# The first adaLN columns of a decoder trunk: summed on VectorE, or multiplied on TensorE as they land

## The reference, cut to what matters

```python
c_act = jax.nn.silu(c)
for l in range(DEPTH):
    cond = c_act @ w_ada[l] + b_ada[l]
    sh_a, sc_a, ga_a, sh_m, sc_m, ga_m = [v[:, None, :] for v in jnp.split(cond, 6, axis=-1)]
    h = rmsnorm(x, g_mix[l]) * (1.0 + sc_a) + sh_a
    z = h @ w_in[l] + b_in[l]
    ...
```

## Time and profile before

| what | value |
|---|---|
| median of 3 runs | 3387.36 us (3386.69 to 3388.49) |
| the profiled execution's own time | 3386.8 us |
| its span | 3385.0 us |
| mean granted TensorE clock | 0.984 |
| TensorE busy | 3240.5 us, 96% |
| VectorE busy | 1612.0 us, 48% |
| GpSimd busy | 1338.4 us, 40% |
| ScalarE busy | 787.6 us, 23% |

### The profile page before, as it was taken

How to read it: one execution, slowest core, us unless ns; L and a number is a source line. 1 busy time by engine, 2 the same in 40 slices (tenths; PEclk the granted TensorE clock), 3 DMA queues, 4 the chain that set the end, 5 groups by cost and what they waited for, 6 DMA issues and landing times.

```text
span 3385.0 us, 38776 instructions
## 1 busy us (share of the span) xinstructions
PE 3240.5 (96%) x15455; PEld 2643.7 (78%) x15485; DVE 1612.0 (48%) x2087; ACT 787.6 (23%) x1331; POOL 1338.4 (40%) x1327
## 2 busy tenths in 40 slices
PE   5999998998899999999999999989979999999999
PEld 4888886676688888888878888867658888888887
DVE  6643245887546433232375333568764532222224
ACT  2100113666212000000120001256751310000002
POOL 2433331333464444444444333313334644444443
PEclk7999999999999999999999999999989999999999
DMA  6434631000522221111143355200015211111112
GB/s 230 133 106 131 187 80 33 1 1 1 193 75 88 75 72 54 50 50 50 50 145 99 113 154 152 59 16 1 1 38 175 75 45 50 50 50 48 46 50 81
DMA packets 293371, 263.02 MB, mean 78 GB/s; under 512 B 10315, under 2 KB 273735, under 8 KB 292680
## 3 DMA queue, kind: packets, MB, share of 16 engines
q1 hardware_dynamic: 278354, 206.61, 20.6%
q10 hardware_dynamic: 14838, 53.94, 4.2%
HBM read 222.76 MB, written 30.41 MB: 75 GB/s over the span
## 4 chain that ended last, share of the span: by engine, by line
PE 88%; DVE 7%; ACT 2%; issue 2%; POOL 0%; ACTq 0%; DVEq 0%; POOLq 0%
PE lin L1045 75%; PE aux L1255 2%; DVE pTL L1839 2%; PE pv L1269 2%; DVE negm L1833 2%; PE lin L1231 1%; PE pv L1270 1%; PE lin L1232 1%; PE pv L1120 1%; PE lin L1210 1%; ACT pTH L1522 1%; PE lin L1065 1%; PE lin L1066 1%; PE lin L1067 1%; DVE acc L835 1%
## 5 line engine op out<-in xcount | busy, mean ns | idle before, releaser
L1016 POOL TENSOR_SCALAR whi<-wraw 128x512 fp32r<-128x512 f32 x504 | 411.1, 816 | 1511.0 <-PE lin L1045 1430.4
L1018 POOL TENSOR_TENSOR wlo<-wraw,whi 128x512 fp32r<-128x512 f32 x504 | 739.2, 1467 | 42.1
L1045 PE MATMUL lin<-hH,whi 128*128 128x512 f32 x2176 | 674.7, 391 | 0.0
L1045 PE MATMUL lin<-hL,whi 128*128 128x512 f32 x2176 | 671.2, 390 | 0.0
L1045 PE MATMUL lin<-hH,wlo 128*128 128x512 f32 x2176 | 670.8, 389 | 0.0
L1045 PEld LDWEIGHTS lin<-hH,wlo 128*128 128x128 f32 x2176 | 408.7, 188 | 86.0
L1045 PEld LDWEIGHTS lin<-hL,whi 128*128 128x128 f32 x2176 | 408.7, 188 | 85.5
L1045 PEld LDWEIGHTS lin<-hH,whi 128*128 128x128 f32 x2176 | 405.9, 188 | 82.6 <-issue 0.8
L1886 DVE SCALAR_TENSOR_TENSOR xT<-lin,adac,xT 128x1024 f32<-128x1024 f32 (+1 forms) x164 | 189.2, 1154 | 525.1 <-PE lin L1045 524.2
L996 POOL TENSOR_SCALAR prob<-prob,fac 128x640 f32<-128x640 f32 (+7 forms) x256 | 184.5, 721 | 466.9 <-DVE fac L1823 448.9
L1921 DVE TENSOR_TENSOR tmp<-tmp 128x1024 f32<-128x1024 f32 x64 | 137.2, 2143 | 432.1 <-ACT tmp L1576 431.9
(11 more groups left out here) (249 smaller groups left out, 3902.6 us busy)
## 6 DMA issues: line engine op xcount, KB each, us to landing
wraw<-in_w_ff SPq DMA_DIRECT2D x134, 512.0 KB, 3.8
wraw<-in_w_ada SPq DMA_DIRECT2D x80, 512.0 KB, 3.8
wraw<-in_w_in SPq DMA_DIRECT2D x78, 512.0 KB, 5.1
wraw<-in_w_o SPq DMA_DIRECT2D x24, 512.0 KB, 3.7
adar<-in_w_ada SPq DMA_DIRECT2D x16, 512.0 KB, 11.2
x_keep<-xT ACTq DMA_DIRECT2D x4, 2048.0 KB, 8.9
mix_keep<-tmp ACTq DMA_DIRECT2D x16, 512.0 KB, 3.5
gate_keep<-ropes ACTq DMA_DIRECT2D x16, 512.0 KB, 6.6
```

What stands on the lines that cost most here:

```text
L1016: pool.tensor_scalar(high, raw, 1.0, 1.0, ALU.mult, ALU.mult).then_inc(w_hi, 1)
L1018: pool.tensor_tensor(wlo[:, SLOT[n], hf], raw, high.bitcast(F32), ALU.subtract).then_inc(w_split, 1)
L1045: mm = pe.matmul(lin[c % 2][:, hf], w, m(k)[:, hf], start=first, stop=last)
```

## The change

VectorE no longer forms `acc`; that tile, its semaphore and the helper `ada` are gone. TensorE multiplies each piece as it lands: for every k, 8 matmuls with the 128x128 blocks of the piece as the stationary operand and `cT[:, k:k+1]` as the moving one, accumulating in PSUM (bank 0 for half 0, bank 1 for half 1). The first four pieces of half 0 come before `spread_rms`, the other four and all of half 1 behind it. `adar1` now signals in pairs too, and its first four pieces are loaded ahead of the first two weight tiles. `dense` runs only the first half of the k steps for both parts, then the second half of the one and of the other. `cmp_done` becomes one semaphore for both layers.

```diff
-            [("first", [P, 2, SEQ], F32), ("crow", [P, P], F32), ("mid", [P, 2 * SEQ - P], F32), ("acc", [P, 2, SEQ], F32),
+            [("first", [P, 2, SEQ], F32), ("crow", [P, P], F32), ("mid", [P, 4 * SEQ - P], F32),
...
-        adar_in = [[sem(f"adar{h}_in{i}") for i in range(n)] for h, n in enumerate((4, 2))]
+        adar_in = [[sem(f"adar{h}_in{i}") for i in range(4)] for h in range(2)]
...
-            ada(adar0, 0, adar_in[0])
+            ada(adar0, 0, adar_in[0], 0, KC)
+            ada(adar1, 1, adar_in[1], 0, 4)
             for n in range(2):
                 load_tile(sp, n)
-            ada(adar1, 1, adar_in[1])
+            ada(adar1, 1, adar_in[1], 4, KC)
...
             pe.transpose(pv[:, 1, 0:P], vecs[:, :], ident[:, :]).then_inc(par_t, 1)
+            begin_columns(pe, 0, 0, 4)
             for h in range(2):
                 spread_rms(pe, 0, h)
-            for h in range(2):
-                begin_columns(pe, h)
-
-        def begin_columns(pe, h):
-
-            pe.wait_ge(acc_made, h + 1)
-            for s in range(2):
-                for i in range(4):
-                    at = s * KC + 4 * h + i
-                    mm = pe.matmul(pv[:, 0, at:at + 1], acc[:, h, s * 512 + i * P:s * 512 + (i + 1) * P], ones[:, 0:1],
-                                   start=True, stop=True)
-            mm.then_inc(p_col, 1)
+            begin_columns(pe, 0, 4, KC)
+            begin_columns(pe, 1, 0, KC)
+
+        def columns_of(h):
+
+            return pv[:, h, 256 * h:256 * h + 2 * KC]
+
+        def begin_columns(pe, h, lo, hi):
+
+            for k in range(lo, hi):
+                if k % 2 == 0:
+                    pe.wait_ge(adar_in[h][k // 2], 32)
+                for s in range(2):
+                    for i in range(4):
+                        at = s * KC + 4 * h + i
+                        w = (adar0, adar1)[h][:, k, s * 512 + i * P:s * 512 + (i + 1) * P]
+                        mm = pe.matmul(columns_of(h)[:, at:at + 1], w, cT[:, k:k + 1], start=k == s == i == 0,
+                                       stop=k == KC - 1 and s == 1 and i == 3, skip_group_check=True)
+            if hi == KC:
+                mm.then_inc(p_col, 1)
...
-            def ada(h, k):
-                w, total = (adar0, adar1)[h][:, k, :], acc[:, h, :]
...
-            ada(0, 0)
             norm_reciprocal(dve, 0, None)
             for h in range(2):
                 norm_diag(dve, 0, h)
-            for k in range(1, KC):
-                ada(0, k)
             modulation(0)
...
                 norm_low(dve, 0, None, k - 1)
-                ada(1, k - 1)
             norm_low(dve, 0, None, 3)
-            for k in range(3, KC):
-                ada(1, k)
             modulation(1)
...
-                    for k in range(kk):
+                    together = kk // 2 if beside else 0
+                    turns = [(k, parts) for k in range(together)] + [(k, [x]) for x in parts for k in range(together, kk)]
+                    for k, here in turns:
...
-                        for c, s, r, j in parts:
+                        for c, s, r, j in here:
...
-                act.wait_ge(cmp_done, 1)
+                act.wait_ge(cmp_done, 2 * layer + 1)
```

More of the change, by code:

```diff
@@ L319, in trunk @@
             [("hH_", [P, KC, SEQ], F32R), ("hN", [P, KC, SEQ], F32)])
-        (qS, kwH, kwL, ksH, ksL), (_, cmp_k1, blk, w2, pe_rows, _, rotated, cmp_v1), (cvH, cvL), (mxH, mxL), (hidH, hidL), (_, crow, _, acc, posr, posf, adar1), (_, rope, rf), (outb,) = region(
+        (qS, kwH, kwL, ksH, ksL), (_, cmp_k1, blk, w2, pe_rows, _, rotated, cmp_v1), (cvH, cvL), (mxH, mxL), (hidH, hidL), (_, crow, _, posr, posf, adar1), (_, rope, rf), (outb,) = region(
             "r_m", 2 * KC * SEQ,
@@ L404, in trunk @@
         x_in = [sem(f"x_in{i}") for i in range(4)]
-        adar_in = [[sem(f"adar{h}_in{i}") for i in range(n)] for h, n in enumerate((4, 2))]
+        adar_in = [[sem(f"adar{h}_in{i}") for i in range(4)] for h in range(2)]
         c_in, pos_in, par_in = sem("c_in"), sem("pos_in"), sem("par_in")
         p_small, p_vec, p_act, p_tr, p_ev = sem("p_small"), sem("p_vec"), sem("p_act"), sem("p_tr"), sem("p_ev")
-        p_sq, acc_made, p_col, rope_out = sem("p_sq"), sem("acc_made"), sem("p_col"), sem("rope_out")
+        p_sq, p_col, rope_out = sem("p_sq"), sem("p_col"), sem("rope_out")
         raw_in = [sem(f"raw_in{i}") for i in range(RAW)]
@@ L414, in trunk @@
         lin_free = [sem(f"lin_free{i}") for i in range(2)]
+        cmp_done = sem("cmp_done")
         par_t, x_made, x_back = sem("par_t"), sem("x_made"), sem("x_back")
@@ L543, in parameters, with ada_part @@
             dve_then(dve, dve.tensor_scalar(qbias[:, :], cols[:, qr:qr + 4], SCALE, None, ALU.mult))
-        def ada_part(dve, lo, hi):
-            dve_then(dve, dve.tensor_tensor(adac[:, lo:hi], pv[:, 0, lo:hi], cols[:, R_ADA + lo:R_ADA + hi], ALU.add))
+        def ada_part(dve, lo, hi, from_=pv[:, 0, :]):
+            dve_then(dve, dve.tensor_tensor(adac[:, lo:hi], from_[:, lo:hi], cols[:, R_ADA + lo:R_ADA + hi], ALU.add))
         def mod(dve, n, lo=0, hi=KC):
@@ L679, in begin_sync, with ada @@
                 sp.dma_start(xin[:, t, :], a["x"][0, t * P:(t + 1) * P, :]).then_inc(x_in[t // 2], 16)
-            def ada(into, h, sems):
-                for k in range(KC):
+            def ada(into, h, sems, lo, hi):
+                for k in range(lo, hi):
                     src = a["w_ada"][0, k * P:(k + 1) * P, 0:2 * D].rearrange("p (s n) -> p s n", s=2)
@@ L843, in modulation @@
                 for s in range(2):
-                    ada_part(dve, s * KC + 4 * h, s * KC + 4 * h + 4)
+                    ada_part(dve, s * KC + 4 * h, s * KC + 4 * h + 4, columns_of(h))
                 mod(dve, 0, 4 * h, 4 * h + 4).then_inc(p_vec, 1)
                 dve.wait_ge(p_vec, 3 + h)
-            ada(0, 0)
             norm_reciprocal(dve, 0, None)
@@ L904, in layer_programs @@
             z_made, aux_done, aux_free, rope_made, blk_made = (lsem(s) for s in ("z_made", "aux_done", "aux_free", "rope_made", "blk_made"))
-            hid_sig, hid_silu, cmp_done, cmp_made = (lsem(s) for s in ("hid_sig", "hid_silu", "cmp_done", "cmp_made"))
+            hid_sig, hid_silu, cmp_made = (lsem(s) for s in ("hid_sig", "hid_silu", "cmp_made"))
             rope_sum, rope_hi, v_hi, vc_lo = (lsem(s) for s in ("rope_sum", "rope_hi", "v_hi", "vc_lo"))
@@ L1470, in scalar @@
                 rope_high("q2")
-                act.wait_ge(cmp_done, 2)
+                act.wait_ge(cmp_done, 2 * layer + 2)
                 act.activation(vcmp[:, :, 0:HD], pv[0:NC, 0, 256:256 + 2 * HD].rearrange("p (g c) -> p g c", g=NKV),
```

## The result

| kernel | median | runs | ratio to before, 95% interval |
|---|---|---|---|
| before | 3387.81 us | 7 (3386.54 to 3391.07) | |
| changed | 3399.64 us | 7 (3394.96 to 3401.19) | 1.0032 (1.0023 to 1.0041) |

The change costs 11.8 us, where 10.0 were forecast. The profiled execution took 3399.64 us with a span of 3397.7, 12.7 above the span before.

A forecast was written before the change was run, and what follows sets the result against it. TensorE's stream was taken to bound the kernel through its dense start: 12.1 - 2.5 + 0.4 = +10.0 us on 3386.8 gives 3396.8, plus 0.6 for the median, 3397.4 us; range 3391 to 3402, 8 in 10.

The forecast's parts named there:

- What bounds it: TensorE's stream: the end moves only with the first dense product's start, 62.8 us before the change.
- The price of a pass: One-column matmul pass on TensorE: 0.214 us at the low clock, 0.11 us at the high; 256 passes needed.
- The clock: TensorE's opening: clock falls at about 21.55 us, then stays low for the columns; 256 passes: 28 us high, 55 low.
- A: Rival: high clock holds through the opening's columns, dense start 13.7 us earlier, 3372.1 us in all; chance 0.08.
- B: Rival: clock high until the eight adar0 pieces end at 35.0 us, then low; no change, 3387.4 us; chance 0.06.
- C: Rival: a weight load costs 0.11 us at either clock level, dense start 12.7 us earlier, 3374.7 us; chance 0.02.
- The sum before the clock terms: Opening on TensorE: columns from 19.0 us put the dense start at 74.9 instead of 62.8 us, +12.1 us.
- the moment of the fall: Opening on TensorE: clock drops at about 21.55 us as before, leaving 23 column passes at the high level.
- The spreading's raise: Norm's 512-column spreading amid the columns may raise the clock briefly: gain of 0 to 3.4 us, taken as 2.5.
- The dense product's slow beginning: Clock rises only some time into the first dense product, 3.1 us before the change; -1.6 to +1.5, taken as +0.4.
- The range: Whole kernel's time: 3391 to 3402 us, 8 in 10; calculated ends 3391.1 and 3401.9 us.
- What costs nothing: Opening: reordered loads, k-step order, h chunks and POOL's splits all hidden or without waits, adding no time.

The follow-up runs named there:

- e2: Changed kernel with every column product of adar1 done twice, 128 more one-column passes into PSUM columns nobody reads: 3426.45 us (one run).
- e4: The split: changed kernel with column products for half 0 only, VectorE summing half 1 meanwhile: 3375.65 us, ratio to before 0.9964; timed again, 3377.46 us.
- e5: Changed kernel with operands exchanged: cT's column stationary, 512 columns of the piece moving into a PSUM row, later turned into columns: 3378.89 us, ratio to before 0.9973.
- e3: Changed kernel with a useless 512-column bf16 matmul behind each pair of passes except the last piece's, 120 in all: 3390.36 us, ratio to before 1.0004.
- e7: Half 0 as rows on TensorE, half 1 summed on VectorE, all adar1 pieces loaded ahead of the two weight tiles: 3372.02 us, ratio to before 0.9950.
- e1: Changed kernel with VectorE's sums restored, keeping only the reordered loads and order of k steps: 3387.49 us, ratio to before 0.9997.
- e6: Changed kernel with half 0 as rows on TensorE (vector stationary, matrix moving) and half 1 summed on VectorE: 3377.32 us, ratio to before 0.9968.

## Why the prediction was right, and where not

- **What bounds it:** right. The dense start moved by 10.4 us and the end by 12.7; e2 moved the one by 27.6 and the other by 26.7 against the changed kernel, e4 both by 12.5 and 12.2 the other way against the kernel before.
- **The price of a pass:** right. 0.213 us in 192 passes (forecast 0.214) at the low level. At the high one an estimate gives 0.11, as forecast: behind the fall, from 24.06 to 28.80 us, 22 of the first 64 passes fit at 0.213, so 42 took the 4.59 us before it. The other form, e5's rows, costs 1.73 us a piece there.
- **The clock:** right, and it was the step that decided. What the two places in the trace of before showed, one-column groups that neither raised nor kept it, held for 41 us without a gap, from 32.4 to 73.2 (e2: 68). e3 and e5 show that it is the clock and not the form. Rivals A, B and C are out: the clock was low, in the second part of half 0 too, and a pass took 0.213 us at it. The Trainium skill's "activity releases the throttle" ("TensorE: Matmul & The Clock Gate", Part 1) would have misled here if taken for any work: 68 us of weight loads with one column each ran at 0.50 throughout.
- **The sum before the clock terms:** 12.1 for the dense start, measured 10.4 and 11.8 in two profiles. What was off is the moment of the fall: I kept it at 21.55 us, it came at 24.1 and at 21.9, and each us at the high level saves about one. Against that the columns began 0.5 and 0.2 us later than the 19.0 that I took.
- **The spreading's raise,** taken at -2.5: 0 in both profiles of the changed kernel, 3.1 to 3.3 us off the columns in both of the split. The ends of 0 and 3.4 were right; the value was a choice between them, and the largest term of the miss. The run at 3394.96 us lies 4.7 below the median, more than such a raise gives; it has no profile, and what it had is open.
- **The dense product's slow beginning,** taken at 0.4 more: 1.1 more in the first profile (5.4 against 3.1 us).
- **Luck:** the terms missed by more than their sum. The span grew by 12.7 where 10.0 were forecast: the missing raise is +2.5, the slow beginning +0.7, what came later +1.2, and the late fall of the clock -1.7. The median grew by 11.8, 0.9 less than the profiled spans.
- **The range:** its low end names a clock that falls 2 us later, but its sum, 3387.4 + 12.1 - 6.8 - 1.6, leaves that out; with it (about -1.9) the end is 3389.2. The fall did come 2.5 us later in the first profile. The result lies far from this end either way.
- **Missed:** the 1.2 us that the moved opening costs at the end of the attention and later. I had passed the shift on unchanged. The path that TensorE never waits on from 100 to 450 us says nothing of the clock's low stretches behind it. By the copy of layer 1's parameters (1456.5 us before; 1468.4 changed, 1444.4 in e4, 1448.3 in e5, 1441.4 in e7) against the dense start, 0.3 to 2.2 us (changed kernel 1.5) are lost between the two, the slow beginning among them.
- **What costs nothing:** right for the load order and the k turns (e1), for the h chunks and POOL's splits (VectorE ended half 0 at 56.9, POOL at 41.7, both far ahead of 73).

## What to carry to other kernels

Price a matrix-vector product on TensorE by what moves: here, with the matrix stationary, a piece of 128x1024 took 3.40 us at a clock that the passes didn't keep up; with the vector stationary and the matrix moving it took 1.73 us, at twice the clock. Before moving work to a faster engine, look whether the slower one could do half of it while it waits: here VectorE was idle from 24 to 46 us, and sharing gave 11 to 13 us, and 16.6 with the rows and the earlier landings, where moving all lost 12.

## What I had not expected of the hardware

- Where the opening ends changes the clock's low stretches hundreds of microseconds later: a second one appeared at 870.7 us, where the kernel before had one, and e1, whose dense product starts only 1.2 us sooner, has three there.
- VectorE's fp32 multiply-adds took 1.64 us in the mean beside POOL's splits and 1.34 with all but the last clear of them (e6: four in 6.58; e7: six in 8.06), so the order of the loads, by that and by the landing itself, decided 4 us of the sum's end (44.6 against 40.6 us).
- A bf16 matmul of 512 columns behind two fp32 passes added 0.13 us to their 0.22, more than the 0.11 that I had allowed for.
